# VectorE in place of GpSimd for ten additions to x in the output projection of a two-block transformer

## The reference, cut to what matters

```python
mod = silu_c @ w_ada[l] + b_ada[l]
shift_m, scale_m, gate_m, shift_f, scale_f, gate_f = jnp.split(mod, N_MOD, axis=-1)
...
mix = jnp.concatenate([o_diff, o_mla], axis=-1) @ w_out[l]
x = x + gate_m[:, None, :] * mix
h = modulate(rmsnorm(x, g_norm_ffn[l]), shift_f, scale_f)
f = jnp.square(jax.nn.relu(h @ w_ff1[l])) @ w_ff2[l]
x = x + gate_f[:, None, :] * f
```

## Time and profile before

| What | Value |
|---|---|
| Median of 3 runs | 1995.99 us (1993.28 to 1996.25) |
| The profiled execution's own time | 1993.64 us |
| Its span | 1991.5 us |
| TensorE busy | 1931.8 us (97%) |
| VectorE busy | 1319.1 us (66%) |
| ScalarE busy | 950.2 us (48%) |
| GpSimd busy | 135.5 us (7%) |
| Granted clock over the span | 0.99 |

### The profile page before, as it was taken

The page is one execution under the profiler, slowest core; times in us unless marked ns, Lnnn a source line. Parts: engine busy times, 40 slices in busy tenths (PEclk is TensorE's granted clock), DMA queues, the critical chain, the costliest instruction groups (busy, mean ns, idle before and its releaser), DMA issues.

```text
span 1991.5 us, 24912 instructions
## 1 busy us (share of the span) xinstructions
PE 1931.8 (97%) x9258; PEld 1605.8 (81%) x9258; DVE 1319.1 (66%) x2075; ACT 950.2 (48%) x1456; POOL 135.5 (7%) x99
## 2 busy tenths in 40 slices
PE   7899999987999999999999999989999999999999
PEld 4478788766888788888888889889998888888887
DVE  4798888889889765555555556577677454555554
ACT  2554566634554344344434455465555444444442
POOL 0000000011000110100110031110000010100000
PEclk9999999998999999999999999999999999999999
DMA  8998785697988755565555546444545465656544
GB/s 344 366 409 335 242 281 206 216 340 258 371 303 330 283 183 186 195 220 185 194 190 190 180 172 207 156 139 149 175 148 169 149 212 190 191 194 188 196 171 179
DMA packets 128970, 447.79 MB, mean 225 GB/s; under 512 B 14289, under 2 KB 14673, under 8 KB 128465
## 3 DMA queue, kind: packets, MB, share of 16 engines
q1 hardware_dynamic: 124928, 433.74, 62.1%
q0 software_dynamic: 1712, 7.87, 1.1%
q10 hardware_dynamic: 2210, 4.61, 0.6%
HBM read 441.96 MB, written 4.19 MB: 224 GB/s over the span
## 4 chain that ended last, share of the span: by engine, by line
PE 89%; DVE 4%; DMA 3%; issue 2%; ACT 2%; POOL 0%; ACTq 0%; SPq 0%; DVEq 0%; POOLq 0%
PE g L1603 27%; PE g L1604 27%; PE g L1597 27%; PE pT L1622 1%; PE pS L1622 1%; PE g L1614 1%; DVE wlo L1953 1%; DMA raw_wide<-in_w_ada 1%; ACT whi L1735 1%; PE pO L1674 1%; DMA raw<-in_w_mem_kv 1%; DVE raw L1958 1%; PE pS L1692 0%; DMA raw<-in_w_out 0%; PE pT L1635 0%
## 5 line engine op out<-in xcount | busy, mean ns | idle before, releaser
L1953 DVE TENSOR_TENSOR wlo<-raw,whi 128x1024 fp32r<-128x1024 f32 (+3 forms) x550 | 653.8, 1196 | 477.4 <-ACT whi L1735 450.2
L1735 ACT ACTIVATE whi<-raw 128x1024 fp32r<-128x1024 f32 (+3 forms) x550 | 551.5, 1006 | 629.3 <-PE g L1604 565.5
L1603 PE MATMUL g<-whi,lhsA_hi 128*128 128x512 f32 (+4 forms) x1840 | 686.7, 375 | 8.4 <-DVE wlo L1953 8.2
L1604 PE MATMUL g<-wlo,lhsA_hi 128*128 128x512 f32 (+4 forms) x1840 | 685.3, 374 | 0.0
L1597 PE MATMUL g<-whi,lhsA_lo 128*128 128x512 f32 (+4 forms) x1840 | 479.2, 382 | 14.8 <-issue 5.7
L1603 PEld LDWEIGHTS g<-whi,lhsA_hi 128*128 128x128 f32 x1840 | 348.3, 189 | 66.2 <-DVE wlo L1953 10.9
L1604 PEld LDWEIGHTS g<-wlo,lhsA_hi 128*128 128x128 f32 x1840 | 348.3, 189 | 54.5
L1597 PEld LDWEIGHTS g<-whi,lhsA_lo 128*128 128x128 f32 x1840 | 329.5, 190 | 69.6 <-issue 17.1
L1603 PE MATMUL g<-whi,lhsF_hi 128*128 128x512 f32 x512 | 199.5, 390 | 0.0
L1604 PE MATMUL g<-wlo,lhsF_hi 128*128 128x512 f32 x512 | 199.4, 389 | 0.0
L1953 DVE TENSOR_TENSOR wlo<-region,whi 128x1024 fp32r<-128x1024 f32 (+1 forms) x102 | 127.8, 1260 | 83.6 <-ACT whi L1735 81.9
(11 more groups left out here) (272 smaller groups left out, 1533.5 us busy)
## 6 DMA issues: line engine op xcount, KB each, us to landing
raw<-in_w_ff SPq DMA_DIRECT2D x182, 512.0 KB, 4.3
raw<-in_w_in SPq DMA_DIRECT2D x158, 512.0 KB, 4.1
raw<-in_w_ada SPq DMA_DIRECT2D x141, 512.0 KB, 5.2
region<-in_w_ff SPq DMA_DIRECT2D x74, 512.0 KB, 4.3
raw<-in_w_out SPq DMA_DIRECT2D x60, 512.0 KB, 5.0
raw<-in_w_in SPq DMA_DIRECT2D x80, 384.0 KB, 3.1
region<-in_w_ada SPq DMA_DIRECT2D x36, 512.0 KB, 6.5
region<-in_w_in SPq DMA_DIRECT2D x18, 512.0 KB, 9.2
```

Of the source, the lines that this page charges most:

```text
L1603: eng.matmul(o, x, p.hi[:, c], start=False, stop=False)
L1604: ins = eng.matmul(o, x, p.lo[:, c], start=False, stop=p.last and kk == 1)
L1735: eng.activation(p.hi, p.raw, ACT.Copy).then_inc(p.hi_done[0], 1)
L1953: eng.tensor_tensor(p.lo, p.raw, p.hi.bitcast(F32), ALU.subtract).then_inc(p.lo_done[0], 1)
```

## The change

The additions of units 0, 1 and 2 and those of the two kept halves are done by VectorE, as those of unit 3 were. The gated products, their buffers and the squares are the same. The semaphore on which the readers wait is VectorE's in place of GpSimd's, and the planner takes the step's cost from VectorE's entry.

```diff
@@ add_kept
             tm = pick(tmps)
-            k, ka = mark("gated"), mark("added_p")
+            k, ka = mark("gated"), mark("added")
             step("gate_rows", tm.ap, r.ap[:, t, :], j, tok, tm.after, g_t, k)
-            step("add_rows", t, j, tm.ap, k, x_tok[j], "pool", ka)
+            step("add_rows", t, j, tm.ap, k, x_tok[j], "dve", ka)
             tm.release(ka)
@@ the loop over the output units
         stats_now()
-        add_in(got, j, True, lambda j=j: gate(0, j), "dve" if j == 3 else "pool")
+        add_in(got, j, True, lambda j=j: gate(0, j), "dve")
         if j + 2 in kept:
             add_kept(j + 2)
```

## The result

| | Before | After |
|---|---|---|
| Median | 1993.93 us (1992.22 to 1996.25, 16 runs) | 1998.18 us (1995.32 to 2001.23, 16 runs) |
| The profiled execution | 1993.64 us, span 1991.5 | 1996.98 us, span 1995.2 |

The ratio is 1.0022, 95% interval 1.0014 to 1.0029. The changed kernel is slower by about 4.3 us, where 2.5 us less was forecast. The forecast's 1993.5 stood on a median of three runs (1995.99); over sixteen runs the same kernel's median is 2.1 us lower, so the ratio is what counts.

The account below looks back on a forecast made before the run. TensorE, busy 97% of the span, was taken as the bound, so only its stops could shrink. Gains of 0.1 + 2.4 = 2.5 us against the median 1995.99 gave 1993.5 us, range 1989.5 to 1998.5.

Parts of the forecast that it names:

- Part 1: Additions' own time on VectorE: 0.69 us each, 1.33 with a gate; ten add 6.9 us.
- Part 2: VectorE instructions stretched beside GpSimd's additions return to free times: 8.2 us back, VectorE's net -1.3 us.
- Part 3: Where this lands in units 0 to 2: TensorE gains 0.1 us; VectorE is 1.0 us ahead after unit 2.
- Part 4: The planner's reordering: four dot products in place of five between unit 2's and unit 3's gates.
- Part 5's first half: Stop behind unit 3: the last dot product's load comes sooner, so unit 3's gates start 2.4 us earlier.
- rival B: Only three dot products stay ahead of unit 3's gates, which wait for TensorE alone; gain 3.7 us, 1992.3; chance 0.16.
- The bound for five dot products: Stop behind unit 3: if all five dot products stay ahead of unit 3's gates, the gain is 1.1 us.
- The tail and the transposes: Behind unit 3's gates: everything moves with them, as VectorE's tail and TensorE's 6.2 us of transposes wait for nothing else.
- Rival C: Transposes behind unit 3 escape the low clock after a shorter stop; up to 3.1 us more gain, 1990.4; chance 0.06.
- Part 5's second half: The moved dot product, done later in 600 to 680, costs nothing; without cover, 1.15 us at a spread-gate wait.
- E: Gain given back at the spread gates' waits: moved dot product and changed order cost 1 to 3 us; 1996.0; chance 0.08.
- D: Stretch in VectorE's stage comes from load traffic and isn't given back; slower, 1998.9, up to 2002.9; chance 0.10.

Follow-up runs that it names:

- run 1: The changed kernel with its additions on VectorE but booked by the planner at GpSimd's cost, keeping the instruction order of before; ratio 0.9992 to the kernel before.
- run 2: The kernel before, additions still on GpSimd but booked at VectorE's cost, giving the instruction order of after; ratio 1.0033 to the kernel before.
- run 5: The changed kernel with group 19's remaining dot products forced into the middle of the sixth half unit; ratio 0.9981 to the kernel before.
- run 3: The changed kernel with the planner's margin for late dot products at 4.5 us in place of 3.5; ratio 0.9995 to the kernel before.
- run 6: The changed kernel without twelve of the sixteen dot products of groups 15 and 19; ratio 0.9967 to the kernel before.
- run 10: The same kernel as run 5, run again beside the kernel before with group 19 forced too; ratio 0.9984 to the kernel before, median 1989.31 us.
- run 8: As run 1, with margin 4.5 us and no dot product let in from unit 3's three feed-forward fetches on; ratio 0.9992 to the kernel before.

## Why the prediction was wrong

The prediction has the way to the restart right, with its sizes too low. The sum fails at a term that was set to nothing.

- **Part 1** is right: 0.69 for an addition, 1.33 for a gate with it.
- **Part 2** is right: all stretched instructions are back at their free times. The forecast net was -1.3 us of VectorE's busy time; the page shows -0.8 over the whole span. One piece of its evidence says nothing: the two gates from PSUM at 431.73 lie ahead of GpSimd's first addition (435.67). The gate that does lie beside one is in the last section. The half of the Trainium skill's rule that spoke against the change (Perfetto Trace Analysis, Optimizing Scalar/DVE Operations) doesn't decide here. Moving work off a saturated VectorE isn't worth it where GpSimd slows it by more than the work: with the list held, VectorE gets through the stage sooner (runs 1 and 2).
- **Part 3** was too careful. The first late dot product was to end at 464.3, VectorE 1.0 us ahead; it starts at 459.79 and ends at 461.01, 3.3 us sooner. Taking off the 1.55 us of the earlier x leaves 1.7, so VectorE is 2.7 us ahead. The gates of units 1 and 2 were held at 447.7 and 459.3; they start at 444.99 and 455.99 and wait for nothing, 1.2 and 1.8 us sooner with the earlier x taken off. So what one unit gives is carried into the next. The first stop stays (2.52 against 2.35), as forecast.
- **Part 4** is right in the stage, to the instruction: one dot product ahead of the feed-forward fetches, three behind, four in place of five.
- **Part 5's first half** has its mechanism right and its size low: -2.4 forecast, -3.6 measured. It inherits Part 3's 1.7 us: the last dot product's load goes out sooner, and its end (465.46) and that of the product (465.32) fall together. That is rival B's size with the forecast's order. The bound for five dot products was 1.1, and run 1, which has five, gives 2.3. The tail and the transposes (6.07 us against 6.21) are as forecast. Rival C's 3.1 us isn't there: the first eight transposes take 2.05 us in both kernels, where eight take 1.05 at 548.69 before.
- **Part 5's second half is the step that failed:** "I cost it at nothing", with its fallback of 1.15 us between 600 and 680. Two things were missed. The first deadline for late dot products is not the spread gates but group 19 for the norm's last columns, at 558, which had 1.2 us to spare. And I followed the planner through the stage only, while its smaller margin also changes the order behind it: the group is finished only when the list has to have it, and the three pairs that covered a 6.8 us tail aren't there any more. In place of 1.15 us the moved dot product and the order behind it cost 9.6 us at that one place: 0.8 of waiting for `mods` and 6.4 of the uncovered tail, which make the 7.2 us stop, and 2.4 of low clock behind it. Run 2 has the stop with the list alone, and run 5 loses it with that one place mended.
- **The rivals.** E had the kind (given back later, by the moved dot product and the changed order), but its place was wrong (no wait of TensorE is left between 600 and 680) and its price of 1 to 3 us was a third of the real one at most. D, the slower rival, fell with Part 2. That the range's upper end of 1998.5 holds the median of 1998.18 is luck: it doesn't follow from the sum (1994.8 and 1.5 are 1996.3), it leans towards a D that didn't happen, and it stands on the high median of three runs. Laid on 1993.93, the same range ends at 1996.4. The chance of 0.07 for slower by over 0.2% was too small, since the changed list was priced only where it was read.
- **A reading.** VectorE's 10.00 us busy are those of 455 to 465, while the stop begins at 467.46; in 465 to 475 it is 7.82. Nothing hangs on it.

## What to carry to other kernels

Where a program orders its own instructions by modelled costs, a change of engine is two changes: the work, and the list. Print both lists or rerun the order by hand to its end, and look for every deadline behind the stage, starting with the one that has the least to spare in the trace of before; an item that slips past it costs the whole uncovered tail, not its own length. Keep the list fixed in one experiment and the engine in the other, and the loss can be put down to one of them in two runs. A gain that both give at the same place needs one more: the mended list with the old engine.

## What the runs showed of the hardware

GpSimd's additions and VectorE's instructions with both inputs in SBUF hold each other up, and all that VectorE loses comes back without them. They take turns. GpSimd and then VectorE in the kernel before, the first two rows of each instruction by instruction:

```profile
436.92 1.28 POOL L2344 TENSOR_TENSOR region<-region,tmp 128x512 f32<-128x512 f32 x1
438.83 1.65 POOL L2344 TENSOR_TENSOR region<-region,tmp 128x512 f32<-128x512 f32 x1 [0.63 <-DVE tmp L2166]
...
448.49 1.29 POOL L2344 TENSOR_TENSOR region<-region,tmp 128x512 f32<-128x512 f32 x1 [5.77 <-DVE tmp L2166]
```
```profile
437.04 1.72 DVE L2166 TENSOR_TENSOR tmp<-row,region 128x512 f32<-128x512 f32 x1 [4.02 <-issue]
438.67 0.68 DVE L2166 TENSOR_TENSOR tmp<-row,region 128x512 f32<-128x512 f32 x1
...
447.72 1.29 DVE L2166 TENSOR_TENSOR tmp<-g,region 128x512 f32<-128x512 f32 x2
```

The gate at 437.04 starts inside an addition that ends at 438.20, and lasts until 438.76, which is 0.56 us or about a free gate's time later. The gate at 438.67 starts first and takes its free 0.68; the addition at 438.83 is the one that is longer. So the engine that comes second waits for the other's instruction. An addition on GpSimd costs the gate 1.04 us here, and VectorE's long instructions 1.07 to 1.1 each, while the same addition takes 0.69 on VectorE: that is how ten of them can be cheaper there. The gates that read PSUM are not held up: the second of the pair at 447.72 lies for 0.5 us beside the addition at 448.49, and both keep their free times.

With GpSimd's additions (run 2), VectorE's four low parts beside them take 4.51 and 4.54 us in pairs, and GpSimd's pairs of additions 2.5 to 3.9; without them (run 1) the pairs of low parts take 2.35. Run 2 in GpSimd's timeline:

```profile
450.81 3.91 POOL L2348 TENSOR_TENSOR region<-region,tmp 128x512 f32<-128x512 f32 x2 [0.63 <-DVE tmp L2170]
```

What I had not priced is the clock behind a stop in a stretch that otherwise runs at full speed. After 7.2 us without a matmul, one of 128x512 takes 0.63 us in place of 0.39, the lower of the two levels in place of the full 2.4 GHz. The stretch 550 to 600 of the changed kernel (length, busy PE, PEld, DVE, ACT, POOL, clock, DMA share, GB/s), where the kernel before has a clock of 1.00:

```profile
550.00:600.00 50.00, 42.78 (x194) 34.94 (x193) 39.40 (x62) 22.57 (x31) 0.00 (x0) 0.90 0.77 267
```

So the 7.2 us stop cost 9.6. Behind unit 3 the transposes start at the lower level in every run, behind 6.62 us as behind 10.36. How long that lasts varies. From the restart to the first pair it takes 6.07 us in the changed kernel and 6.21 in the one before, but 5.14 or 5.15 in runs 2, 3, 6 and 10, all with stops under 7 us, and 6.18 and 6.21 in runs 5 and 8 with the same stop of 6.62. No profile with a stop of 8.99 or more is under 5.60. So a shorter stop can give about a microsecond of clock, and doesn't always. Run 10, TensorE:

```profile
473.12 2.05 PE L1634 MATMUL pS<-region 128*128 128x128 f32 x8 [6.62 <-issue]
...
478.27 1.17 PE L1602 MATMUL g<-whi,lhsA_lo 128*128 128x512 f32 x4
```
